# The head-norm scaling of a delta-rule mixer, moved from one GpSimd operation to eight ScalarE operations per head

## What is computed

```python
def finish(o, z):
    b, h, l, dv = o.shape
    o = rms_norm(jnp.transpose(o, (0, 2, 1, 3)), o_norm_g).astype(z.dtype)
    return (o.reshape(b, l, DN_VAL_DIM) * jax.nn.silu(z)) @ w_out
```

## Time and profile before

| | us |
|---|---|
| median of three runs | 2775.22 |
| lowest and highest of the three | 2774.98, 2782.2 |
| the profiled execution, whole | 2771.29 |
| its span on the core | 2769.6 |
| the eight head calls in the trace | about 185 to 992 |

### The profile page before, as it was taken

One profiled execution on the slowest core, in us unless ns is written; L12 is line 12 of the kernel. 1 busy time (PEld: TensorE's weight loads), 2 busy tenths in 40 slices (PEclk: granted clock), 3 DMA queues, 4 the chain that ended last, 5 costly groups with the idle time before them and its releaser, 6 DMA issues. The chain is left out here.

```text
span 2769.6 us, 39984 instructions
## 1 busy us (share of the span) xinstructions
PE 2234.2 (81%) x16012; PEld 1683.0 (61%) x16012; DVE 1200.7 (43%) x2260; ACT 548.4 (20%) x1196; POOL 127.9 (5%) x89
## 2 busy tenths in 40 slices
PE   4489889889889769596667885887888577888997
PEld 1356666656666634173356663877875466777886
DVE  2355665665665610312423785442452454421101
ACT  0034334333344310001201222001001311100000
POOL 0000000000000000000000000000000122100000
PEclk8599999999999989797788995988999787899998
DMA  6110110110110021440022211000002211133443
GB/s 267 65 47 1 47 48 1 47 47 1 47 47 1 2 91 61 182 156 0 0 102 91 92 61 50 1 24 24 1 23 76 80 46 58 64 127 120 153 175 124
DMA packets 50329, 183.58 MB, mean 66 GB/s; under 512 B 5744, under 2 KB 7152, under 8 KB 49648
## 3 DMA queue, kind: packets, MB, share of 16 engines
q1 hardware_dynamic: 50160, 181.18, 17.6%
HBM read 180.11 MB, written 1.05 MB: 65 GB/s over the span
## 5 line engine op out<-in xcount | busy, mean ns | idle before, releaser
L347 PE MATMUL banks<-u,w_ring 128*128 128x256 f32 x1664 | 379.4, 387 | 13.5 <-PEq L190 13.5
L699 PE MATMUL banks<-u,w_ring 128*128 128x512 f32 x768 | 356.0, 601 | 14.0 <-PEq L190 14.0
L347 PEld LDWEIGHTS banks<-u,w_ring 128*128 128x128 f32 x1664 | 319.1, 195 | 60.4 <-issue 17.8
L699 PEld LDWEIGHTS banks<-u,w_ring 128*128 128x128 f32 x768 | 141.2, 192 | 144.7 <-issue 141.6
L484 PE MATMUL banks<-u,w_ring 128*128 128x256 f32 (+1 forms) x640 | 159.5, 413 | 23.4 <-PEq L190 21.0
L484 PEld LDWEIGHTS banks<-u,w_ring 128*128 128x128 f32 x640 | 126.1, 198 | 56.3 <-issue 39.7
L484 PE MATMUL banks<-gated,w_ring 128*128 128x512 f32 (+1 forms) x384 | 139.6, 526 | 11.5 <-PEq L2279 10.0
L484 PEld LDWEIGHTS banks<-gated,w_ring 128*128 128x128 f32 x384 | 73.4, 192 | 77.2 <-issue 74.0
L726 DVE SCALAR_TENSOR_TENSOR acc<-raw,hc,acc 128x512 f32<-128x512 f32 x128 | 96.2, 752 | 4.5
L484 PE MATMUL banks<-ffn,w_ring 128*128 128x256 f32 x352 | 77.9, 385 | 3.0 <-PEq L190 3.0
L426 ACT ACTIVATE sq<-h 128x256 f32<-128x256 f32 (+1 forms) x48 | 18.8, 472 | 304.3 <-PEq L190 304.3
(11 more groups left out here) (467 smaller groups left out, 3720.9 us busy)
## 6 DMA issues: line engine op xcount, KB each, us to landing
w_ring<-in_w SPq DMA_DIRECT2D x323, 512.0 KB, 6.1
h<-in_h SPq DMA_DIRECT2D x2, 2048.0 KB, 7.8
const_base<-in_const SPq DMA_DIRECT2D x1, 1216.0 KB, 9.9
const_part<-in_const SPq DMA_DIRECT2D x1, 1024.0 KB, 5.0
out<-u SPq DMA_DIRECT2D x1, 1024.0 KB, 4.8
const_part<-in_const SPq DMA_DIRECT2D x1, 640.0 KB, 4.4
const_part<-in_const SPq DMA_DIRECT2D x1, 512.0 KB, 3.5
w_rows<-in_rows SPq DMA_DIRECT2D x1, 512.0 KB, 5.6
```

What stands on the lines that cost most here:

```text
L347: last = nc.tensor.matmul(out, lhs[k], rhs[k], start=(k == 0), stop=(k == n - 1))
L699: mm = nc.tensor.matmul(self.places[m % len(self.places)][:, :], st.slot(m)[:, P * k:P * k + P], u[:, k, :], start=(k == 0), stop=(k == KT ...
```

## The change

The GpSimd multiplication is removed. In its place ScalarE waits for `o_root` and multiplies the eight tiles of 128x128 one by one, each by its own column of `ms`, in place; the last raises `o_norm`. In a call with `more=True` they stand behind `decays` 3 and ahead of the gate's four operations; in the last call they follow the square directly.

```diff
                     inverse_root(nc, pool, C, ms[:, :], s["o_mean"], s["o_root"])
-                    o3 = od[:, 0, :, :].rearrange("p t (j e) -> p (t j) e", j=2)
-                    link(nc.gpsimd.tensor_tensor(o3, o3, ms[:, :].unsqueeze(2).to_broadcast([P, 2 * TT, P]), ALU.mult), s["o_norm"])
                     if not more:
                         link(nc.gpsimd.memset(lower[:, :, :, half(0)], 0.0))
...
                         front.tanh(act, link, 3)
                         front.decays(act, link, 3)
+                    act.wait_ge(s["o_root"], 1)
+                    for t in range(TT):
+                        for j in range(2):
+                            out = od[:, 0, t, P * j:P * j + P]
+                            link(nc.scalar.activation(out, out, ACT.Copy, scale=ms[:, 2 * t + j:2 * t + j + 1]),
+                                 s["o_norm"] if t == TT - 1 and j else None)
+                    if more:
                         act.wait_ge(s["z_ready"], 1)
                         front.gate(act, link, 0)
                         front.gate(act, link, 1)
```

## The result

The changed kernel took 2800.9 us in the median of seven executions against 2775.22 for the kernel before, also seven; the ratio is 1.0084, 95% interval 1.0058 to 1.0109. So it is slower, as forecast, and the interval holds the forecast's 1.006, but the median lies 3 us above the range. One of the seven executions, the one that was profiled, ran at a mean granted TensorE clock of 0.40 and took 5896 us; it is left out of the ratio (the median of the other six is 2800.4), and the profile shown here is of the same kernel in a repeat, labelled `again`.

What follows compares the result with a forecast made beforehand. The prediction took ScalarE's decays of chain 3, then VectorE's work to the last gating, to bound calls with a front. Seven times 2.20 plus 1.6 gave 17.0 us, so 2775.2 became 2792.2; range 2784 to 2798.

Steps and rivals of the forecast that it cites:

- The removed operation gives nothing by itself: In seven calls GpSimd's 1.90 us is off the path; VectorE's freed 0.87 us only waits for decays 3.
- One tile 0.43, eight 3.46: ScalarE's added scaling: 0.40 us plus 0.03 for the link per tile, 3.46 us for eight.
- TensorE 0.14 later, at the lower clock, 1.94 us: In calls with a front, transposes start 0.14 us after scaling and take 1.94 us at 1.2 GHz, not 1.04.
- The new tail: End of each call with a front, after decays 3: last gating moves from 287.98 to 290.18, 2.20 us a call.
- The last call 1.6: In the last call ScalarE ends scaling at 990.39 instead of GpSimd's 988.80: 1.6 us, all on the path.
- The sum: All eight head calls: 15.4 us for seven calls plus 1.6 for the last, 17.0 us in all.
- VectorE's column: Rival: VectorE ends the calls with a front and scaling is hidden, giving 2770.7 us; chance 0.04.
- the next call: Rival: transposes keep TensorE's clock up, next call starts faster, at most 6 us in all, 2786; chance 0.15.
- the dearer tile: Rival: ScalarE's scaling costs 0.49 us a tile, calls lose 2.9 each and the last 2.3, 2798; chance 0.08.
- The 3.9 us: Offset by which the median of runs stands above the profiled execution, 2775.2 against 2771.29 us before the change.

Runs made afterwards that it cites:

- reorder: Kernel before, GpSimd still multiplying, with ScalarE's fourth tanh ahead of the decays of chain 2 and VectorE's fourth silu behind chain 1; ratio 0.9993.
- early: Kernel before with ScalarE scaling in two idle stretches, fourth tanh and silu moved earlier, VectorE multiplying in the last call; ratio 0.9968, repeated 0.9988.
- double: The change plus eight more ScalarE scalings into an unread scratch tile, right ahead of the eight that count; ratio to the kernel before 1.0159.
- pairs: The change, with ScalarE scaling the first value head's four tiles and releasing TensorE, then the second's four; ratio to the kernel before 1.0054.
- last_only: The change only in the last call, GpSimd still multiplying in the seven calls with a front; ratio to the kernel before 1.0006.
- unchanged: The kernel before without an edit, submitted like an experiment; ratio to the kernel before 0.9989.

## Why the prediction was right and where it failed

- *The removed operation gives nothing by itself.* Right. VectorE got its 0.87 us back in each of seven calls and waited for the decays with it; `reorder` against `early` shows what it is worth on the path. The Trainium skill (SBUF — State Buffer, Who interferes with whom) has it that the later of GpSimd and a two-port VectorE instruction is blocked fully; the step went from 1.36 to 0.49 us wherever GpSimd's operation was gone and stayed where it was kept, and where it was long it ended 0.28 us after GpSimd (275.99 and 275.71), so the runs agree.
- *One tile 0.43, eight 3.46.* Right: 0.401 each, eight in 3.44, and `double` adds 3.46.
- *TensorE 0.14 later, at the lower clock, 1.94 us.* Right in all eight calls: the transposes' fastest is 417 ns, against 272 at the full clock. The reasoning was wrong twice, and the errors cancelled. It counted TensorE's idleness from 282.68, which is where the old transposes end; but these are the work that moves, and what stands ahead of them ends at 281.80. So the idle time is 5.59 us and not 4.7, and 5.59 is what all seven calls of `again` have. And the earlier trace rows does not hold for all calls. The row of the seventh begins 5.0 us behind TensorE's last work, not 4.2; at 4.2 the granted clock there was still 1.00, and so it was in the fourth, which does not lie between 0.50 and 0.69. The windows are of the kernel before, calls 4 and 7, then of `again`, the same calls, just ahead of the transposes at 611.98 and 932.71:

```profile
600.80:601.30 0.50, 0.00 (x0) 0.00 (x0) 0.34 (x2) 0.00 (x0) 0.00 (x0) 1.00 0.00 0
914.40:914.90 0.50, 0.00 (x0) 0.00 (x0) 0.47 (x2) 0.00 (x0) 0.00 (x0) 1.00 0.00 0
```
```profile
611.10:611.60 0.50, 0.00 (x0) 0.00 (x0) 0.00 (x0) 0.47 (x2) 0.00 (x0) 1.00 0.00 0
611.70:611.90 0.20, 0.00 (x0) 0.00 (x0) 0.00 (x0) 0.17 (x2) 0.00 (x0) 0.50 0.00 0
931.90:932.40 0.50, 0.00 (x0) 0.00 (x0) 0.00 (x0) 0.47 (x2) 0.00 (x0) 1.00 0.00 0
932.50:932.70 0.20, 0.00 (x0) 0.02 (x1) 0.00 (x0) 0.17 (x2) 0.00 (x0) 0.50 0.00 0
```

  In `again` the fall in these two calls came less than 0.4 us ahead of the transposes. `pairs`, where TensorE was idle for 3.86 us, began its first group at the upper level in four of the seven calls (the first transpose takes 300 ns there and 447 to 449 in the other three). So the lower clock in all seven was in part luck.
- *The new tail.* Forecast 6.39 (2.20 more), measured 6.59 (2.40 more). The term that was too small is the one from TensorE's start to the last gating, taken from the last call as 1.19 + 1.60: there VectorE writes to a fixed place; in the loop's calls a register step of 0.07 us stands ahead of each gating (twelve in the trace, two in each of the six), which I read as the address being computed, and the same stretch is 1.32 + 1.65. The seventh call, outside the loop, has none and keeps the 1.19, as does the last call in `last_only`.
- *The last call 1.6.* Right: 1.56.
- *The sum.* Forecast 17.0, by the tails 18.4, by the ratios of three measurements 16.4, 19.4 and 23.3.
- *The rivals.* VectorE's column did not end the call (the waits show it), the next call did not start faster, and the tile was not dearer. None of the three took place.
- *The step that failed is the range.* Its upper end, 2798, was the dearer tile alone; for the level of the runs it allowed two us below and nothing above. The mis-sized tail accounts for 1.4 of the 8.7 us between the forecast of 2792.2 and the measured 2800.9 (18.4 by the tails against 17.0). The other 7.3 are in no tail. The same kernel, measured three times beside the kernel before, had medians 25.7, 20.7 and 15.2 us above it; the six executions that the first ratio counts span 22 us (2785.9 to 2807.7), the three times of before that were known already spanned 7, and the stages without an edit are 1961 us in one trace of the change and 1949 in the other. So 2800.9 was a high draw of a scattered number, and that scatter had no place in the upper bound. By these numbers a median of a few executions needs some 6 us on each side beside the terms, an estimate made with the result known; with it, 2778 to 2804 would have held 2800.9. In the stage at 1.93 ms the longer traces are those with the lower granted clock; what lowers it stays open.
- *The 3.9 us* between the profiled execution and the median play no part in the forecast, which is 2775.2 + 17.0 either way; the trace of before was merely one of the short ones (`unchanged` has 2776.6 on the span for 2769.6).

## What to carry to other kernels

A move to an idle engine is priced by what stands last ahead of the barrier, not by the engine's share: the same eight operations cost 2.4 us a call behind the last decays and nothing visible in the tail in two holes of 2.3 us earlier in the same list. Before moving an operation, write down for its new engine what it will stand behind and what waits for it, and see whether the engine whose burden is lifted ends anything at all. When the time hangs on how long an engine has been idle, count from the last work that stays, not from the work that the change itself moves. And put the scatter of the executions at hand into the range before the bounds of the terms.

## What the runs showed of the hardware that was not expected

TensorE's granted clock differs between executions of one program in stages that are far from any edit: 0.93 or 0.88 over the same 1140 matmuls, worth 6.3 us of 196, and 65.9 against 63.3 us in the stage ahead of the head calls (0.86 in `unchanged`, 0.93 in the first trace of the same kernel). What sets it was not tried and stays open.
